# Layer 1's feed-forward on one Trainium2 core: the way down by seven products of halves, woven into the gate and up products

## The reference, cut to what matters

```
def swiglu(a, wg, wu, wd):
    return (jax.nn.silu(a @ wg) * (a @ wu)) @ wd
...
h = h + g1[:, None] * m_lat
f_lat = modulate(rmsnorm(h, norm_ffn_g[layer]), sh2[:, None], sc2[:, None])
h = h + g2[:, None] * swiglu(f_lat, ffn_w_gate[layer], ffn_w_up[layer], ffn_w_down[layer])
```

## Time and profile before

| | us |
|---|---|
| median of 3 runs (3217.99 to 3225.23) | 3218.37 |
| the profiled execution | 3220.7 |
| its span, first to last instruction | 3218.9 |
| TensorE busy | 3071.1 (95%) |
| GpSimd busy | 2286.9 (71%) |
| VectorE busy | 1953.8 (61%) |
| ScalarE busy | 1104.8 (34%) |

### The profile page before, as it was taken

How to read it: one execution, slowest core, us unless ns; L and a number is a source line. 1 busy time by engine, 2 the same in 40 slices (tenths; PEclk the granted TensorE clock), 3 DMA queues, 4 the chain that set the end, 5 groups by cost and what they waited for, 6 DMA issues and landing times. The chain is left out here.

```text
span 3218.9 us, 44354 instructions
## 1 busy us (share of the span) xinstructions
PE 3071.1 (95%) x14438; PEld 2501.2 (78%) x14438; DVE 1953.8 (61%) x2546; ACT 1104.8 (34%) x1899; POOL 2286.9 (71%) x2297
## 2 busy tenths in 40 slices
PE   7999998998989999999899999999999999999999
PEld 6777876878877888888677777777777778888887
DVE  6585665777874455454535567777765764454454
ACT  4322775134620110110333456776762410110010
POOL 3584765763498888888623268888887688888885
PEclk9999999999999999999999999999999999999999
DMA  6367322557621111111203541111114211112112
GB/s 238 108 206 202 76 58 110 181 176 262 213 83 59 46 52 59 46 52 60 103 30 106 153 129 48 40 41 48 38 28 144 66 40 59 47 51 61 50 45 85
DMA packets 134922, 297.74 MB, mean 92 GB/s; under 512 B 36448, under 2 KB 69472, under 8 KB 134688
## 3 DMA queue, kind: packets, MB, share of 16 engines
q1 hardware_dynamic: 121632, 252.89, 25.4%
q10 hardware_dynamic: 13184, 43.52, 4.4%
HBM read 251.68 MB, written 44.63 MB: 92 GB/s over the span
## 5 line engine op out<-in xcount | busy, mean ns | idle before, releaser
L1590 POOL TENSOR_TENSOR a_pl<-a_p,a_ph 128x512 fp32r<-128x512 f32 x320 | 450.4, 1429 | 97.4 <-ACT a_p L1535 92.4
L164 PE MATMUL ps<-a_q,a_k 97*128 97x512 f32 x960 | 270.2, 394 | 0.5 <-POOL a_v L1602 0.5
L1534 ACT ACTIVATE a_ph<-ps 128x512 fp32r<-128x512 f32 x320 | 192.5, 601 | 174.1 <-PE ps L164 173.3
L1436 DVE TENSOR_REDUCE a_top<-ps 128x1 f32<-128x512 f32 x256 | 173.3, 688 | 94.7 <-PE ps L1353 94.7
L164 PE MATMUL ps<-hidden,whi 128*128 128x512 f32 x704 | 218.7, 392 | 7.2 <-POOL wlo L1897 4.3
L164 PE MATMUL ps<-mixed_hi,l_whi 128*128 128x512 f32 (+1 forms) x544 | 206.0, 379 | 10.9 <-POOL l_wlo L139 4.7
L3080 POOL TENSOR_TENSOR l_wlo<-l_raw,l_whi 128x512 fp32r<-128x512 f32 x154 | 200.2, 1300 | 12.8
L164 PEld LDWEIGHTS ps<-a_q,a_k 97*128 97x128 f32 x960 | 177.8, 189 | 37.6 <-POOL a_v L1602 1.4
L164 PE MATMUL ps<-mixed_lo,l_whi 128*128 128x512 f32 (+1 forms) x544 | 205.0, 377 | 0.0
L164 PE MATMUL ps<-mixed_hi,l_wlo 128*128 128x512 f32 (+1 forms) x544 | 204.9, 377 | 0.0
L2533 DVE SCALAR_TENSOR_TENSOR residual<-ps,mod,residual 128x512 f32<-128x512 f32 x176 | 132.1, 751 | 110.4 <-PE ps L164 110.4
(11 more groups left out here) (425 smaller groups left out, 8946.5 us busy)
## 6 DMA issues: line engine op xcount, KB each, us to landing
l_raw<-in_w_ffn SPq DMA_DIRECT2D x132, 512.0 KB, 3.7
raw<-in_w_ffn SPq DMA_DIRECT2D x66, 512.0 KB, 3.6
l_row<-in_mod_t ACTq DMA_DIRECT2D x32, 512.0 KB, 4.4
f_vraw<-in_mod_t ACTq DMA_DIRECT2D x24, 512.0 KB, 4.1
a_k<-scratch_k SPq DMA_DIRECT2D x32, 320.0 KB, 6.6
f_raw<-in_w_in SPq DMA_DIRECT2D x16, 512.0 KB, 5.4
l_raw<-in_w_out SPq DMA_DIRECT2D x16, 512.0 KB, 4.4
l_shared_row<-in_mod_t ACTq DMA_DIRECT2D x16, 512.0 KB, 6.2
```

Source lines behind the costliest of these rows:

```text
L164: last = nc.tensor.matmul(out, a, b, start=at == 0, stop=at == n - 1)
L1436: nc.vector.tensor_reduce(top[:, q:q + 1, c], e.ps[:, bank:bank + BANK], AX.X, ALU.max).then_inc(s["auxr"], 1)
L1534: nc.scalar.activation(ph[:, kk % 2, c], b, ACT.Exp).then_inc(s["exp"], 1)
L1590: nc.gpsimd.tensor_tensor(pl[:, kk % 2, c], p[:, kk % 2, c], ph[:, kk % 2, c].bitcast(F32), ALU.subtract).then_inc(s["pl"], 1)
```

## The change

The way down of a pair (256 hidden features to 1024 outputs, 1024 tokens) is also done by seven products of halves, `d0` to `d6`, of 12 matmuls each: four row tiles x 3. Each runs in two parts of 6 matmuls, one behind each of the fourteen gate and up products `g0` to `g13`. The four banks 4 to 7 hold the four row tiles; an odd-numbered way-down product is added onto the even one before it, and VectorE adds or subtracts what stands in the bank to one quarter of `h` after each (`reads`). These sums are no longer scaled by the gate vector, so `h` starts the loop at zero: the residual is written to DRAM scratch first (`spill`), `h` is cleared on ScalarE, and at the end the residual is read back into the place of `hi` (`back`), where the scaled sum and the scaled last pair are added (`last_pair`, `scaled_row`). The high parts of the weights move from GpSimd to ScalarE (`weight_high`), the settling operations go, GpSimd keeps the low parts and makes twelve sums. Gate and up products use three weight slots and four banks instead of six and six, the way down two slots (3 and 4). Way-down weights are loaded in halves of 256 KB into places of their own. `rms` and `rstd` move into `total`. Semaphores that are waited on ahead of their first event are raised at the start (`P_FREE` 3, `D_FREE` 8, `O_FREE` 4).

```diff
+            extra = sb(f"{name}_raw_extra", [128, BANK], F32)
+            t2_ = sb(f"{name}_t2", [128, BANK], F32)
...
+            hid = {(f, c): hid_plain[:, 2 * f + 1, c * BANK:(c + 1) * BANK] for f in range(2) for c in range(2)}
+            t2 = t2_[:, :]
+            op_h = [hh[:, 0, 0:BANK], hh[:, 0, BANK:2 * BANK], wh[:, 5, :]]
+            op_l = [hl[:, 0, 0:BANK], hl[:, 0, BANK:2 * BANK], wl[:, 5, :]]
...
+            PRODUCTS, DOWNS, HALVES, SUMS, MOVED = 14, 28, 21, 12, 4
+            ORDER = ("g0", "d0", "g1", "g2", "d1", "g3", "g4", "d2", "g5", "g6", "d3", "g7", "g8", "d4", "g9", "g10", "d5", "g11", "g12", "d6", "g13")
+            position = {x: y for y, x in enumerate(ORDER)}
+            WSUMS = ("gs3", "gs1", "gs2", "ds1", "ds2", "gs4", "ds3", "us3", "us1", "us2", "ds4", "us4")
             QUARTERS = (0, 0), (1, 1), (1, 0), (0, 1)
-            pbank = [x % 6 * BANK for x in (0, 1, 2, 3, 4, 5, 0, 1, 2, 3, 4, 5, 0, 1)]
-
-            def slot(pos):
-                return (pos + 4) % 6
+            GP = (1, 2, 6, 7, 5, 4, 3)
+            DP = (0, 1, 0, 1, 0, 1, 2, 0)
+            pbank = [x * BANK for x in (0, 1, 2, 3, 0, 1, 2, 3, 0, 1, 2, 3, 1, 2)]
+            G_FREE, D_FREE, P_FREE, O_FREE = 3, 8, 3, 4
+            LAST = pairs - 1
...
+            def slot(x):
+                if x[0] == "g":
+                    return int(x[1:]) % 3
+                return (3, 4, 3, 4, 3, 4, 3)[int(x[1:])]
...
+            SOURCE = {**{f"g{x + 7 * y}": "abascds"[x] for x in range(7) for y in range(2)},
+                      **{f"d{x}": "xxyzzzy"[x] for x in range(7)}}
...
+                def loads(i, more):
+                    sp.wait_ge(s["wsum"], i * SUMS + summed("gs4"))
+                    first_row(i, 4)
+                    sp.wait_ge(s["half"], i * HALVES + made("d2"))
+                    down_fourth(i)
+                    sp.wait_ge(s["half"], i * HALVES + made("g5"))
+                    second_row(i, 5)
+                    if more:
+                        sp.wait_ge(s["wsum"], i * SUMS + summed("ds4"))
+                        down_first(i + 1)
+                        sp.wait_ge(s["half"], i * HALVES + made("d5"))
+                        down_second(i + 1)
+                    sp.wait_ge(s["wsum"], i * SUMS + summed("us4"))
+                    first_row(i + 1, 0)
+                    sp.wait_ge(s["half"], i * HALVES + made("g12"))
+                    second_row(i + 1, 1)
+                    if more:
+                        sp.wait_ge(s["half"], i * HALVES + made("d6"))
+                        down_third(i + 1)
...
+                sp.wait_ge(s["res"], NJ)
+                for k in range(KT):
+                    sp.dma_start(e.scratch["h"][k, :, :], h[:, k, 0:LAT]).then_inc(s["spill"], 16)
+                sp.wait_ge(e.split_done, first.number(0, 3) + 1 + RING)
+                first_row(0, 0)
+                down_first(0)
+                second_row(0, 1)
+                down_third(0)
+                down_second(0)
+                with each(sp, LAST - 1) as i:
+                    loads(i, True)
...
+                def weights(i):
+
+                    low_part(i, "g0")
+                    low_part(i, "d0")
+                    low_part(i, "g1")
+                    pool.wait_ge(s["r1"], i * 32 + 16)
+                    combine(i, "gs3", "s", "a", "c", ALU.subtract)
+                    combine(i, "gs1", "c", "c", "d", ALU.add)
+                    taken(i, "g0")
+                    combine(i, "gs2", "a", "c", "a", ALU.subtract)
+                    low_part(i, "g2")
+                    pool.wait_ge(s["dy"], i * 32 + 16)
+                    pool.wait_ge(s["dz"], i * 16 + 16)
+                    combine(i, "ds1", "y", "y", "z", ALU.add)
+                    taken(i, "d0")
+                    combine(i, "ds2", "x", "y", "x", ALU.subtract)
+                    low_part(i, "d1")
+                    low_part(i, "g3")
+                    taken(i, "g3")
+                    combine(i, "gs4", "s", "b", "a", ALU.subtract)
+                    low_part(i, "g4")
+                    low_part(i, "d2")
+                    low_part(i, "g5")
+                    low_part(i, "g6")
+                    low_part(i, "d3")
+                    low_part(i, "g7")
+                    low_part(i, "g8")
+                    taken(i, "d3")
+                    combine(i, "ds3", "z", "z", "x", ALU.subtract)
+                    low_part(i, "d4")
+                    pool.wait_ge(s["r1"], i * 32 + 32)
+                    taken(i, "g6")
+                    combine(i, "us3", "s", "a", "c", ALU.subtract)
+                    combine(i, "us1", "c", "c", "d", ALU.add)
+                    taken(i, "g7")
+                    combine(i, "us2", "a", "c", "a", ALU.subtract)
+                    low_part(i, "g9")
+                    low_part(i, "g10")
+                    pool.wait_ge(s["dy"], i * 32 + 32)
+                    taken(i, "d4")
+                    combine(i, "ds4", "z", "x", "y", ALU.subtract)
+                    low_part(i, "d5")
+                    taken(i, "g10")
+                    combine(i, "us4", "s", "b", "a", ALU.subtract)
+                    low_part(i, "g11")
+                    low_part(i, "g12")
+                    low_part(i, "d6")
+                    low_part(i, "g13")
...
+                    for d in (3, 5):
+                        for m in range(4):
+                            nc.gpsimd.tensor_tensor(rows_of(d, m), rows_of(d, m), rows_of(1, m), ALU.add).then_inc(s["fsum"], 1)
+                    for m in range(4):
+                        pool.wait_ge(s["scaled"], m + 1)
+                        pool.wait_ge(s["back"], 16 * 16)
+                        nc.gpsimd.tensor_tensor(back(4 + m, 1), back(4 + m, 1), rows_of(1, m), ALU.add).then_inc(s["fsum"], 1)
...
+                def down_products(i, d, x):
+
+                    at, z = slot(f"d{d}"), DP[d]
+                    if x == 0:
+                        pe.wait_ge(s["half"], i * HALVES + made(f"d{d}"))
+                        pe.wait_ge(s["op_lo"], i * 7 + d + 1)
+                    for m in (2 * x, 2 * x + 1):
+                        pe.wait_ge(s["out"], i * DOWNS + 4 * d + m + 1)
+                        w = slice(m * 128, (m + 1) * 128)
+                        for y_, (a, b) in enumerate(((wh, op_h), (wh, op_l), (wl, op_h))):
+                            last = nc.tensor.matmul(e.ps[:, (4 + m) * BANK:(5 + m) * BANK], a[:, at, w], b[z],
+                                                    start=d in (0, 2, 4, 6) and y_ == 0, stop=y_ == 2, skip_group_check=True)
+                        last.then_inc(s["down"], 1)
...
+                    with each(pe, LAST) as i:
+                        for x in range(PRODUCTS):
+                            product(i, x)
+                            down_products(i, x // 2, x % 2)
+                    pe.wait_ge(s["flo"], 4)
+                    pe.wait_ge(s["out"], LAST * DOWNS + O_FREE)
+                    for x, (m, c) in enumerate(FINAL):
+                        pe.wait_ge(s["fw"], 2 * (m // 4) + 2)
+                        if x >= 4:
+                            pe.wait_ge(s["fout"], x - 3)
+                        o, w = (4 + x % 4) * BANK, slice(m % 4 * 128, m % 4 * 128 + 128)
+                        products(nc, e.ps[:, o:o + BANK], [(wh[:, fslot[2 * (m // 4) + z], w], wl[:, fslot[2 * (m // 4) + z], w],
+                                                           fop(z, c, 0), fop(z, c, 1)) for z in range(2)]).then_inc(s["fdown"], 1)
...
+                def weight_high(i, x, sem_=None, count=None):
+                    if sem_ is not None:
+                        act.wait_ge(s[sem_], count)
+                    if x[0] == "g":
+                        g = int(x[1:])
+                        act.wait_ge(s["product"], i * PRODUCTS + (-1, 0, -2)[g] + P_FREE if g < 3 else i * PRODUCTS + g - 2 + P_FREE)
+                    else:
+                        act.wait_ge(s["down"], i * DOWNS + max(int(x[1:]) * 4 - 4, 0) + D_FREE)
+                    nc.scalar.activation(wh[:, slot(x), :], raw_half(SOURCE[x]), ACT.Copy).then_inc(s["half_hi"], 1)
...
+                def operand_high(i, d, of, sem_, count, free_):
+                    act.wait_ge(s[sem_], count)
+                    act.wait_ge(s["down"], free_ + D_FREE)
+                    nc.scalar.activation(op_h[DP[d]], of, ACT.Copy).then_inc(s["op_hi"], 1)
...
+                def iteration(i):
+                    n0, ts = i * DOWNS, i * 4
+                    weight_high(i, "g0", "r0", i * 32 + 16)
+                    weight_high(i, "d0", "dx", i * 16 + 16)
+                    weight_high(i, "g1")
+                    weight_sum(i, "g2", "gs2")
+                    operand_high(i, 1, t2, "tsum", ts + 2 + 16, n0 - 4)
+                    gate_first(i)
+                    weight_sum(i, "d1", "ds2")
+                    weight_sum(i, "g3", "gs3")
+                    weight_sum(i, "g4", "gs1")
```

(109 more changed lines are left out.)

330 lines of the change are left out of this document (139 added, 191 removed).

## The result

The changed kernel takes 3268.42 us in the median of four runs (3264.19 to 3269.07), the kernel before 3221.8 in the runs beside them (3217.99 to 3226.54): a ratio of 1.0142, interval 1.0128 to 1.0156. Slower, as forecast, by 46.6 us against the 35 of the sum.

What follows compares the result with a forecast made beforehand. TensorE bounds the kernel, but the changed pass waits on a ScalarE-GpSimd chain up to `d1`. 1.3 + 9 x 2.5 + 5 + 6.5 = 35 us on the median of 3218.37 gives 3253; range 3216 to 3278, 8 in 10.

Steps and rivals of the forecast that it cites:

- the sum: Whole kernel: 1.3 before the loop, 9 x 2.5 in it, 5 for clock, 6.5 after it: 35 us slower.
- The step: One loop pass: 62.3 us against 59.84, 2.5 longer, from a 15.7 us chain up to `d1`; bounds 60.7 to 64.5.
- The saving inside the loop: Loop: 252 matmuls a pass instead of 264, 57.12 us if nothing stalls, 2.72 less; coming in full had 13%.
- Contention: Chain up to `d1`: four VectorE SBUF operations each delay GpSimd by 0.32, 1.3 us more in a pass.
- the four meetings: Chain up to `d1`: two hidden differences, low half of `d1`'s operand, third difference meet GpSimd; 2.8 us by exclusion rule.
- The second chain: From `d2`'s end to `g9`: 12.4 us plus some 0.5 contention against 12.24 of matmuls; 0.4 us counted per pass.
- The clock: TensorE's granted clock falls after idle gaps of some 2.4 us, in two or three of nine passes: 5 us altogether.
- that rival: Loop: the clock falls in every pass, 2.5 us each, or GpSimd is contested throughout; 3270 us; 18%.
- The lead-in: Before the loop: pass 1 begins at 2653.4, 1.3 us later than today; wrong if outside 2650 to 2657.
- The zeroing: Before the loop: eight clearings of `h` on ScalarE end near 2584 and cost nothing; up to 8 us without cover.
- The tail: After the loop: last read 32.3 us behind the last matmul, 6.5 later; wrong if under 29 or over 35.
- the 6.5 us to the first matmul: After the loop: two high halves, four `fhi` and four contested lows between its last matmul and the next.

Runs made afterwards that it cites:

- experiment 1: Changed kernel with the weights of `d6` in slot 2, so the high half of `d0` no longer waits for the previous pass's last matmul; 3249.8 us.
- experiment 2: Changed kernel with GpSimd making the gate sums `gs3`, `gs1`, `gs2` ahead of the low parts of `d0` and `g1`; 3223.0 us.
- experiment 6: Changed kernel with GpSimd's whole list in order of need and, on ScalarE, `g8`'s high half ahead of `d4`'s operand; 3220.6 us.
- experiment 4: Changed kernel with three of VectorE's hidden differences and the low half of `d1`'s operand done on 8 columns instead of 512; 3249.95 us.
- experiment 8: Changed kernel with three of the last four weight halves in slots freed earlier and the last hidden quarters' halves made inside the last pass; 3266.1 us.

## Why the prediction was right, and by how much it was off

**A pass.** The step held to 0.3 us: 62.3 forecast, 62.6 measured where the clock cost nothing. From the pass's start to `d1` it took 15.7 us, the number of the sum. The saving inside the loop died where the text put it, on the wait of `d0`'s high half for the last matmul and on what stood behind it in the two lists (experiment 1: 2.2 us; experiment 2: all of the lengthening and 0.6 of the saving of 2.72; experiment 6: 1.2 of it). Contention, 1.3 in the sum, was 1.3 (experiment 4), but that the two agree is luck: the sum had four operations at 0.32, the trace has three at 0.45. By the Trainium skill (SBUF — State Buffer, on its two separate sides) one of the two engines blocks for the other's whole instruction; an estimate by that rule gives 2.8 for the four meetings. The trace agrees that both engines' operations get longer when they meet, and the measured price is under half. The second chain's 0.4 was 0.21 seen as idle, and from `d1` to `g9` 27.93 us for 114 matmuls (25.8) and the clock's 1.6: 0.5. Nine passes cost 2.3 more than the sum had for them.

**The clock** was the term most mis-sized: 5 us counted, for falls in two or three passes. It fell in every pass, as that rival said, but not at the rival's price. Where it fell during `g2`, the twelve matmuls took 4.5 us instead of 3.0 and ran into a wait that was there anyway: ahead of `d1` TensorE then idled 0.72 instead of 2.24, and the pass lasted 62.6. Where it fell behind `d1` it cost 1.6, in six of nine passes: 9.8 us. The Trainium skill (TensorE: Matmul & The Clock Gate, on oscillation) warns that a wait which returns with each tile brings the low clock back each time; by the changed kernel's windows that happened here. The two gaps of 2.1 to 2.2 us brought it down in every pass, one of 2.24 (experiment 1) in six of nine, gaps of 1.25 and 1.80 (experiment 4) in one of nine, one of 0.99 (experiment 2) in none.

**The lead-in**: pass 1 began at 2655.4, forecast 2653.4, inside the 2650 to 2657. The zeroing was not quite hidden: it ran from 2577.57 to 2585.2 with the silu behind it, at 2585.13 instead of 2583.53, and the rest of the list was late by that. The lead-in cost 2 us more than the sum had for it.

**The tail** ended at the edge of its own test: last read 35.0 us behind the recorded end of the loop's last matmul (35.3 behind its start), where 32.3 was forecast and 35 the limit. The mis-sized part is the 6.5 us to the first matmul, measured 8.85: three high halves stood behind the last product, not two, and the four lows of VectorE took 1.64 us each beside GpSimd's last low parts and first sums. From there on 26.1 us, forecast 25.8. The 1.4 us that the forecast gave the clock here stands on no row; the clock did read 0.50, the lower level, from 3237.6 to 3242.0 us, but experiment 8 shows VectorE at the limit once TensorE no longer waits, so what the clock cost by itself is not shown.

Sum of the parts: 3.3 + 9 x 2.76 + 9.8 + 9.4 = 47.3, by which the span grew; the forecast had 1.3 + 22.5 + 5 + 6.5.

The four parts all came out above the sum, and no error made up for another between them.

Still open: what keeps the best passes, 58.64 us, 1.5 above the 57.12 of 252 matmuls without a wait; two waits of 0.46 and 0.45 us account for part of it. Open too: whether VectorE's last 28 operations could be cut down, by which the tail would get near the 25.8 of before. No run tried it.

## What to carry to other kernels

When work moves from one engine's list to two, follow each list past every wait: an operation that waits for a slot to come free holds back whatever stands behind it, ready or not, and here moving three sums ahead of it was worth 40 of 47 us, the clock's falls included. Totals of busy time (here 45.5 us of work on GpSimd in a pass, against the 57.1 that TensorE needs) don't show that. A stall of two microseconds on TensorE costs more than itself when the clock falls behind it (1.6 us here), and the fall costs nothing when the slow stretch ends in another wait. A time that looks like a tie can hide a difference outside the change: take the interval inside the trace.

## What was unexpected in the hardware

- A fall of the granted clock (0.62 between 2665 and 2668 us, g2's matmuls) that cost nothing at all, since it spent time that the next wait would have taken.
- Two extra fp32 matmuls in each stall, 1.88 us recorded with a pass no longer than without them, kept the clock at 1.00 and saved 9.8 us in nine passes.
- VectorE's lows with both inputs in SBUF take 0.6 us in a row of four (2.49) when GpSimd is idle, and 1.44 to 1.64 (5.76, 6.57) beside its low parts and sums, while a sum of GpSimd pays 0.45 (1.74 against 1.29).
- The stage ahead of the change, the same code in all these kernels, ended anywhere from 2579.2 to 2589.4 us in their traces; twelve runs of the kernel before spread over 15 us.
